# Recurrent core of a two-block mixer kernel: the next chunk's front steps placed between the steps of the present chunk

## What is computed

```
def step(state, inp):
    r_t, w_t, k_t, v_t, kk_t, a_t = inp
    sa = jnp.einsum('bhvk,bhk->bhv', state, kk_t)
    state = (state * w_t[:, :, None, :]
             - sa[..., :, None] * (kk_t * a_t)[..., None, :]
             + v_t[..., :, None] * k_t[..., None, :])
    return state, jnp.einsum('bhvk,bhk->bhv', state, r_t)
...
_, out = lax.scan(step, state0, tuple(seq_first))
```

## Time and profile before

| | |
|---|---|
| median of 3 runs | 2829.52 us (2829.08 to 2830.18) |
| the profiled execution's own time | 2828.0 us |
| its span, first to last instruction | 2826.2 us |
| mean granted TensorE clock | 0.959 |
| TensorE busy, share of the span | 94% |
| VectorE, ScalarE, GpSimd busy | 41%, 20%, 33% |
| the core's matmuls, first to last start | 409.7 to 647.9 us |

### The profile page before, as it was taken

One profiled execution on the slowest core, in us unless ns is written; L12 is line 12 of the kernel. 1 busy time (PEld: TensorE's weight loads), 2 busy tenths in 40 slices (PEclk: granted clock), 3 DMA queues, 4 the chain that ended last, 5 costly groups with the idle time before them and its releaser, 6 DMA issues.

```text
span 2826.2 us, 35717 instructions
## 1 busy us (share of the span) xinstructions
PE 2644.1 (94%) x15644; PEld 1584.4 (56%) x15644; DVE 1151.9 (41%) x1288; ACT 560.9 (20%) x617; POOL 928.9 (33%) x390
## 2 busy tenths in 40 slices
PE   4869999999899999999998899999889999999996
PEld 1545558886455555555554666776345555555552
DVE  5466666663533310223126665255443220222233
ACT  3225422211211100111003122321131110011102
POOL 0212110000144444444445766101124444444450
PEclk8989999999899999999998999998889999999998
DMA  5432020000011111111113412300001111111101
GB/s 237 164 119 82 20 101 3 3 3 15 30 40 50 54 53 43 45 53 45 62 65 137 58 54 67 119 1 23 30 30 45 53 59 46 44 47 53 59 31 60
DMA packets 44267, 162.65 MB, mean 58 GB/s; under 512 B 4560, under 2 KB 14288, under 8 KB 41168
## 3 DMA queue, kind: packets, MB, share of 16 engines
q1 hardware_dynamic: 38496, 151.21, 16.4%
q10 hardware_dynamic: 5616, 9.17, 1.1%
HBM read 147.77 MB, written 12.58 MB: 57 GB/s over the span
## 4 chain that ended last, share of the span: by engine, by line
PE 87%; DVE 6%; DMA 2%; POOL 2%; issue 1%; ACT 1%; SPq 0%; ACTq 0%; DVEq 0%; POOLq 0%
PE pt L918 17%; PE pt L924 17%; PE pt L921 16%; PE pt L1232 13%; PE pt L561 7%; PE pt L411 3%; PE pt L700 2%; PE pt L1930 2%; PE pt L1936 2%; PE pt L1933 2%; PE pt L344 1%; DVE work L532 1%; DMA work<-in_xT 1%; PE pt L397 1%; PE pt L332 1%
## 5 line engine op out<-in xcount | busy, mean ns | idle before, releaser
L889 POOL TENSOR_TENSOR weights_rounded<-work,cst 128x1024 fp32r<-128x1024 f32 (+1 forms) x120 | 314.8, 2623 | 956.9 <-issue 692.5
L921 PE MATMUL pt<-work,weights_rounded 128*128 128x512 bf16 x1408 | 348.8, 384 | 0.0
L893 POOL TENSOR_TENSOR slots<-work,weights_rounded 128x1024 bf16<-128x1024 f32 (+1 forms) x120 | 337.6, 2813 | 9.4
L921 PEld LDWEIGHTS pt<-work,weights_rounded 128*128 128x128 bf16 x1408 | 125.6, 99 | 183.7 <-issue 66.1
L561 PE MATMUL pt<-work 64*64 64x64 f32 (+5 forms) x4512 | 215.3, 247 | 13.4 <-DVE work L532 12.4
L561 PEld LDWEIGHTS pt<-work 64*64 64x64 f32 (+3 forms) x4512 | 196.7, 144 | 32.3 <-DVE work L532 17.2
L918 PE MATMUL pt<-rounded,weights_rounded 128*128 128x512 f32 x704 | 206.1, 428 | 8.8 <-DVE work L1850 5.2
L918 PE MATMUL pt<-rhs_rounded,weights_rounded 128*128 128x512 f32 x704 | 206.2, 428 | 7.8 <-DVE work L815 4.2
L918 PE MATMUL pt<-hidden_rounded,weights_rounded 128*128 128x512 f32 x704 | 207.5, 427 | 0.0
L1006 DVE SCALAR_TENSOR_TENSOR slots<-pt,par,slots 128x1023 f32<-128x1023 f32 x44 | 56.4, 1283 | 315.7 <-ACT slots L992 315.7
L924 PE MATMUL pt<-hidden_rounded,slots 128*128 128x512 bf16 x704 | 179.9, 387 | 0.0
(11 more groups left out here) (330 smaller groups left out, 3495.0 us busy)
## 6 DMA issues: line engine op xcount, KB each, us to landing
work<-in_w_up SPq DMA_DIRECT2D x88, 512.0 KB, 3.6
work<-in_w_mod SPq DMA_DIRECT2D x11, 2048.0 KB, 8.6
work<-in_w_down SPq DMA_DIRECT2D x32, 704.0 KB, 4.0
slots<-in_w_in SPq DMA_DIRECT2D x31, 512.0 KB, 3.7
slots<-in_w_v SPq DMA_DIRECT2D x10, 512.0 KB, 4.0
work<-in_xT ACTq DMA_DIRECT2D x4, 1024.0 KB, 23.1
x_scratch<-work SPq DMA_DIRECT2D x8, 512.0 KB, 2.7
slots<-in_w_out SPq DMA_DIRECT2D x8, 512.0 KB, 3.4
```

What stands on the lines that cost most here:

```text
L889: did(pool, pool.tensor_tensor(w_hi(n, cols).rearrange("p (k n) -> p k n", n=P), w_raw(n, cols).rearrange("p (k n) -> p k n", n=P), const( ...
L893: did(pool, pool.tensor_tensor(w_lo(n, cols), w_raw(n, cols), w_hi(n, cols).bitcast(F32), ALU.subtract), "ffn_w_split")
L921: pe.matmul(out, top_half(w_hi(n, cols))[:, k * P:k * P + P], rhs_lo(k), start=False, stop=False, skip_group_check=True)
```

## The change

The front steps of chunk `c + 1` (transposes, products, first step, values) no longer stand ahead of that chunk as a block. They are issued one pair at a time between the steps of chunk `c`. TensorE's table `beside` says where: transposes of pair 0 behind the x matmuls of level 0, its products behind the t matmuls of level 0, its first step behind those of level 1; pair 1 likewise at levels 2, 2 and 3; pair 2 at level 4 and, its first step, behind step v of the solve. The values stand behind r and g. VectorE's `beside_x` puts the scores copy of pair 0 behind the masks of level 1, its inverse copy behind those of level 2, pair 1's behind those of levels 3 and 4, pair 2's behind level 4.

From chunk 1 on all pairs use `PT[3]` for the front, so a pair's transposes wait for the inverse copy of the pair before (`inverse_set`). Scores, inverses, token-major copies and values get a second buffer; scores of even chunks lie in slots 45, 46 and 30. These held x for the residual sum. So x for tiles 3 to 7 is loaded once chunk 6 is done. GpSimd clears nine slots, after `lg2` instead of `c8`. Chunk 0's front is a block as before. The number of matmuls, copies and predicated copies is unchanged.

```diff
+        CA2 = (45, 46, 30)
...
+        def scores_at(c, i):
+
+            return w((CA2, CA)[c % 2][i])
+
+        def lower_t(c, i, h, rows, q):
+
+            return scores_at(c, i)[rows, h * 512 + 64 * q:h * 512 + 64 * q + 64]
+
+        def scores(c, i, h, n):
+
+            return scores_at(c, i)[:, h * 512 + n * P:h * 512 + n * P + P]
+
+        def inverse(c, i):
+
+            return w(CB_[i])[:, c % 2 * 256:c % 2 * 256 + 256]
...
+        def front(c, i):
+
+            return PT[i] if c == 0 else PT[3]
...
-            pool.wait_ge(E("pt_filled"), place["c8"] + 1)
-            for s in CA + CC:
+            pool.wait_ge(E("pt_filled"), place["lg2"] + 1)
+            for s in CA + CA2 + CD:
                 did(pool, pool.memset(w(s), 0.0), "core_zeroed")
             for c in range(NC):
                 for i in range(3):
-                    if c > 0:
-                        pool.wait_ge(E("y_done"), 3 * (c - 1) + i + 1)
-                    did(pool, pool.tensor_copy(inverse(i).rearrange("p (x n) -> p x n", x=4),
+                    if c >= 2:
+                        pool.wait_ge(E("solve_done"), 9 * (c - 2) + 6 + i + 1)
+                    did(pool, pool.tensor_copy(inverse(c, i).rearrange("p (x n) -> p x n", x=4),
                                                const("unit").unsqueeze(1).to_broadcast([P, 4, 64])), "inverse_unit")
 
...
+                sequence(0, i)
+            values(0)
             for c in range(NC):
                 tt = slice(c * CH, (c + 1) * CH)
+                if c + 1 < NC:
+                    for i in range(3):
+                        sequence(c + 1, i)
...
+                if c + 1 < NC:
+                    values(c + 1)
...
+            def kept(c, i):
+                dve.wait_ge(E("products_done"), 3 * c + i + 1)
+                V_(dve.copy_predicated(heads(scores_at(c, i)), per_head(keep[:, 0:512], 512), heads(front(c, i)[:, :])),
+                   "scores_kept")
+
+            def first(c, i):
+                dve.wait_ge(E("inverse_unit"), 3 * c + i + 1)
+                dve.wait_ge(E("l_done"), 3 * c + i + 1)
+                V_(dve.copy_predicated(heads(inverse(c, i)), per_head(keep[:, 512:640], P),
+                                       heads(front(c, i)[:, :])[:, :, 0:P]), "inverse_set")
+
+            dve.wait_ge(E("core_zeroed"), 9)
             dve.wait_ge(E("keep_in"), 16)
             dve.wait_ge(E("p_end"), 3)
+            for i in range(3):
+                kept(0, i)
+            for i in range(3):
+                first(0, i)
+            beside_x = {1: (kept, 0), 2: (first, 0), 3: (kept, 1), 4: (first, 1)}
             for c in range(NC):
                 tt = slice(c * CH, (c + 1) * CH)
+                more = c + 1 < NC
                 for i in range(3):
                     V_(dve.tensor_scalar(s_scaled(i), state(i), small(PMID + 8 * i + c), None, ALU.mult))
                     V_(dve.tensor_scalar(s_ended(i), s_scaled(i), small(PEND + 8 * i + c), None, ALU.mult), "state_scaled")
...
                 for n, b in enumerate(LEVELS):
                     for i in range(3):
                         dve.wait_ge(E("x_done"), 15 * c + 3 * n + i + 1)
                         V_(dve.tensor_tensor(heads(xbuf(i)), heads(bank_a(i)[:, 0:P]), per_head(const(f"level{b}"), 64),
                                              ALU.mult), "x_masked")
+                    if more and n in beside_x:
+                        step, i = beside_x[n]
+                        step(c + 1, i)
                     for i in range(3):
                         dve.wait_ge(E("t_done"), 15 * c + 3 * n + i + 1)
+                        t = inverse(c, i)
...
+                if more:
+                    kept(c + 1, 2)
+                    first(c + 1, 2)
...
+            def transposes(c, i):
                 tt = slice(c * CH, (c + 1) * CH)
+                if c > 0 and i == 0:
+                    pe.wait_ge(E("mv_kept"), c)
+                if c > 0 and i > 0:
+                    pe.wait_ge(E("inverse_set"), 3 * c + i)
+                for x, s in enumerate((Z + i, B + i, KK + i, VV + i)):
+                    ins = pe.transpose(front(c, i)[:, x * P:x * P + P], w(s)[:, tt], const("ident"))
+                ins.then_inc(E("transposed"), 1)
+
+            def products(c, i):
+                tt = slice(c * CH, (c + 1) * CH)
+                pe.wait_ge(E("seq_major"), 3 * c + i + 1)
+                for x, s in enumerate((B + i, KK + i)):
+                    for h in range(2):
+                        ins = mm(front(c, i)[:, h * 512 + x * 256:h * 512 + x * 256 + 256], w(s)[half(h), tt],
+                                 both(Z, i, 21, tt)[half(h)])
+                ins.then_inc(E("products_done"), 1)
...
+            def first(c, i):
                 tok = [slice(c * CH + 64 * q, c * CH + 64 * q + 64) for q in range(2)]
...
+                pe.wait_ge(E("scores_kept"), 3 * c + i + 1)
...
+                ins.then_inc(E("l_done"), 1)
+
+            def values(c):
                 if c > 0:
-                    pe.wait_ge(E("mv_kept"), c)
...
                 ins.then_inc(E("mv_done"), 1)
+
+            pe.wait_ge(E("pt_emptied_dve"), ordinal["o2"])
+            pe.wait_ge(E("core_zeroed"), 9)
+            for step in (transposes, products, first):
+                for i in range(3):
+                    step(0, i)
+            values(0)
+            beside = {"x0": (transposes, 0), "t0": (products, 0), "t1": (first, 0), "x2": (transposes, 1), "t2": (products, 1),
+                      "t3": (first, 1), "x4": (transposes, 2), "t4": (products, 2), "v": (first, 2)}
+            for c in range(NC):
+
+                def also(phase):
+                    if c + 1 < NC and phase in beside:
+                        step, i = beside[phase]
+                        step(c + 1, i)
+
                 for n in range(5):
                     for i in range(3):
-                        pe.wait_ge(E("inverse_ready"), 18 * c + 3 * n + i + 1)
+                        if n == 0:
+                            pe.wait_ge(E("inverse_set"), 3 * c + i + 1)
+                            if c > 0:
+                                pe.wait_ge(E("o_kept"), 3 * (c - 1) + i + 1)
+                        else:
+                            pe.wait_ge(E("inverse_ready"), 15 * c + 3 * (n - 1) + i + 1)
...
+                    also(f"x{n}")
                     for i in range(3):
                         pe.wait_ge(E("x_masked"), 15 * c + 3 * n + i + 1)
+                        if n == 0 and c > 0:
+                            pe.wait_ge(E("state_new"), 3 * (c - 1) + i + 1)
...
                         ins.then_inc(E("t_done"), 1)
+                    also(f"t{n}")
...
+                    ins.then_inc(E("solve_done"), 1)
+                also("v")
...
                     ins.then_inc(E("rg_done"), 1)
+                if c + 1 < NC:
+                    values(c + 1)
...
                     sp.wait_ge(E("pt_filled"), place["c8"] + 1)
-                    sp.dma_start(W[:, XP[0]:XP[0] + 5, :], a["xT"][:, 0:5, :]).then_inc(E("x_in0"), 16)
-                if m == 1:
-                    sp.wait_ge(E("pt_filled"), place["lg2"] + 1)
-                    sp.dma_start(W[:, XP[5]:XP[5] + 2, :], a["xT"][:, 5:7, :]).then_inc(E("x_in1"), 16)
+                    sp.dma_start(W[:, XP[0]:XP[0] + 3, :], a["xT"][:, 0:3, :]).then_inc(E("x_in0"), 16)
                 if m == 4:
                     sp.wait_ge(E("pt_emptied_dve"), ordinal["bon2"])
                     sp.wait_ge(E("p_end"), 3)
-                    sp.dma_start(w(XP[7]), a["xT"][:, 7, :]).then_inc(E("x_in2"), 16)
                     woc = EX[:, 0:3, :].rearrange("p a n -> p (a n)").rearrange("p (m n) -> p m n", m=8)
                     for mm in range(8):
                         sp.dma_start(woc[:, mm, :], a["w_out"][mm][:, 640:1024]).then_inc(E("woc_in"), 16)
+                    sp.wait_ge(E("chunk_done"), 3 * NC - 3)
+                    sp.dma_start(W[:, XP[3]:XP[3] + 2, :], a["xT"][:, 3:5, :]).then_inc(E("x_in1"), 16)
+                    sp.dma_start(W[:, XP[5]:XP[5] + 2, :], a["xT"][:, 5:7, :]).then_inc(E("x_in2"), 16)
+                    sp.dma_start(w(XP[7]), a["xT"][:, 7, :]).then_inc(E("x_in2"), 16)
             sp.wait_ge(E("y_c"), 3)
             sp.wait_ge(E("pt_filled"), place["o7"] + 1)
```

More of the change, by code:

```diff
@@ L489, in core_act, with sequence @@
         def core_act(act):
-            act.wait_ge(E("core_zeroed"), 6)
+            def sequence(c, i):
+                act.wait_ge(E("transposed"), 3 * c + i + 1)
+                did(act, act.activation(w(CC[i])[:, c % 2 * 512:c % 2 * 512 + 512], front(c, i)[:, 0:512], ACT.Copy),
+                    "seq_major")
+            def values(c):
+                act.wait_ge(E("mv_done"), c + 1)
+                did(act, act.activation(W[:, CD[0]:CD[2] + 1, c % 2 * 512:c % 2 * 512 + P],
+                                        PT[3][:, 512:896].rearrange("p (i n) -> p i n", i=3), ACT.Copy), "mv_kept")
@@ L502, in core_act @@
```

(32 more changed lines are left out.)

115 lines of the change are left out of this document (40 added, 75 removed).

## The result

| | before | changed |
|---|---|---|
| median | 2828.34 us (2823.18 to 2833.87, 8 runs) | 2845.91 us (2839.02 to 2854.58, 8 runs) |
| ratio, 95% interval | | 1.0064 (1.0048 to 1.008) |
| profiled execution: own time, span | 2828.0, 2826.2 | 2846.58, 2844.8 |
| mean granted clock | 0.959 | 0.962 |
| core, first transposes to the last state update's end | 240.3 us | 265.8 us |

The change makes the kernel 17.6 us slower, which is more than the 0.2% that a measurement can tell. A chunk's period is counted from the end of one chunk's last state update to the end of the next one's; the core's first and last chunk are not counted, since the changed order puts the next chunk's front into the first and has none to put into the last.

The account below looks back on a forecast made before the run. The prediction took TensorE to carry 87% of the chain, with levels where TensorE and VectorE are nearly full. Waits +15, tile shapes +4 and clock +7 made +26 us, giving 2855.5 us, range 2835 to 2875.

Parts of the forecast that it names:

- rival (a): Core: slower by waits and shape changes alone, clock at 2.4 GHz throughout; +11 us, 2840; chance 0.18.
- clock term: Core: new waits double the present six stretches at half clock to twelve, 15.6 us against 8.2; +7 us.
- shape term: Core: tile-shape changes on TensorE go from some 7 to 16 a chunk, 0.1 us for each uncovered one; +4 us.
- the sign: Core: the chunk's period away from half clock should be 31 to 31.7 us in the changed profile.
- The waits: Core: TensorE waits for moved VectorE steps in levels, less the front's 2.3 us; +2.15 us a chunk, +15 in all.
- 8.45 end to end: Levels 1 and 2 laid end to end with moved work and waits: 3.35 and 5.1 us, 8.45 together.
- Outside the core: Clearing and late x loads outside the core: 0 us with cover, at most 9 without it.
- (b): Core: faster, moved work fills TensorE's waits, under 2.3 us of added waits per chunk; 2805 us; chance 0.08.

Follow-up runs that it names:

- e1: Changed kernel with VectorE's six state scalings moved from the chunk's head to the solve part: chunk 31.23 us against 32.38, in all 2842.64 us.
- e2: Changed kernel with the transposes of pairs 1 and 2 one step later, their products and pair 2's first step following: chunk 30.09 us, in all 2828.14.
- e3: Changed kernel with scores copies of pairs 0 and 1 cut from 512 to 64 columns per head, chunks 1 to 7: chunk 30.38 us, in all 2829.16.
- e8: Changed kernel with both scalings moved to the solve part and later transposes of pairs 1 and 2: chunk 28.95 us, ratio 0.9966 to the kernel before.
- e4b: Kernel before plus four dummy matmul calls a chunk with 128x128 weights in the solve, chunks 1 to 7: in all 2841.89 us.
- e6: Changed kernel with both order tables rewritten for more lead behind copies, values behind the chunk's last matmul: chunk 28.15 us, ratio 0.9961 to the kernel before.
- e7: Changed kernel with another pair of order tables, values left in place, scalings behind r and g: 2815.53 us, ratio 0.9967 to the kernel before.
- e5: Kernel before with only nine cleared slots instead of six and the late loads of x: chunk 28.94 us, in all 2829.57 beside 2822.03.
- r1: The changed kernel profiled once more, unchanged: total 2856.81 us against 2846.58 in its first profile, core 266.7 us.
- r2: The kernel before profiled once more, unchanged: cores of the two profiles 240.3 and 240.4 us, stages outside the core 2583.1 us.
- e4a: Kernel before plus four dummy matmul calls a chunk with 64x64 weights, the shape around them, chunks 1 to 7: in all 2825.82 us.

## Why the prediction was right, point by point

Slower was forecast at 0.87, 2855.5 us within 2835 to 2875; it is 2845.91, between the forecast and rival (a) at 2840. The mechanism, waits of TensorE for moved VectorE steps, was right. That +26 for the core came so close to its 25.5 was luck: the clock term was 7 us too high and the shape term 5 too low. The chunk's period shows the second, 32.38 us where 31 to 31.7 was given as the sign.

**The waits (+2.15 a chunk, +15).** Right, in place and size. By the timeline they are 1.31, 0.51 and 1.14 us, forecast as 1.4, 0.5 and 1.15, and e1, e2 and e3 take them away one by one (1.15, 2.29 and 2.00 us a chunk, the last with the gaps of 0.2 between x steps, which were forecast too); e8 shows that the first two add. As a net term the 2.15 was not measured by itself: it is the chunk's 3.45 less the 1.3 by which "issue" grew. The argument from the earlier trace rows, two nearly full engines that hand over to each other, is what the runs bear out.

**The tile shapes (+4).** Mis-sized. "Issue" grew by 1.3 us a chunk, 9 us over seven chunks. I had charged 0.1 us for six of nine new changes. By e4b one costs an estimated 0.15, and nine make 1.35. Levels 1 and 2 show it: from 588.76 to 597.67 they take 8.91 us, and I had laid 8.45 end to end; four changes lie there, into and out of the transposes and the products. The wait hides the change into the transposes, but not the one out of them (0.17 at 595.06), and behind lone products the next weight load comes late by 0.33. The row's 0.17 for every change would have been the better estimate. So was the Trainium skill's rule (TensorEngine Tiling (Array Packing), Key Properties) that changing the tiling mode drains TensorE, under which the term was 7.

**The clock (+7).** Wrong. Twelve spells were forecast from the number and length of the waits; there are five, one double, about as much half clock as before (20.5 us in both). Before, the seven counted periods exceed 7 x 28.93 by 8.0 us, in the changed kernel six exceed 6 x 32.38 by 7.5, so the term is near 0. "Each spell at 1.2 GHz came in a chunk whose TensorE had just stood through those waits" was true, but nearly every chunk stands through them, and it does not say which gets a spell: ten of fourteen inverse-copy waits have none, e1 with fewer waits has more half clock, and e2, e3, e6, e7 and e8 have none in the core behind chunk 0. That removing waits removes spells fits these five and not e1, and e4b has more spells without a new wait for another engine, so the cause is open.

**Outside the core (0).** Right for loads and clearing (e5); the changed kernel's clearing and the first unit copies are through by 383.4 us, well ahead of the core. Not foreseen was that unchanged stages would run some 7 us shorter. With 15 + 9 + 0 = 24 for the terms, the core's +25.5 is nearly accounted for, and the total's 17.6 is that less the stages outside. Those took 2585.9 and 2583.1 us in the two profiles of the kernel before and 2579.0 and 2588.3 in those of the changed one (r1 is 31.5 us over r2 in all), so no shift by the change is shown: what differs is mostly their time at half clock. The distance between forecast and median is thus for the most part a matter of stages that the prediction rightly put at no cost, and of their scatter.

**The rivals.** (a), waits without half clock, was close in total for another reason: spells remained, the shapes cost more, and the outside gave something back. (b), faster, was wrong for this table and right for another. Its condition was under 2.3 us of added waits a chunk with the copies in idle VectorE time; e6 and e7 reach it by giving most copies a step of lead, and e8's period, 28.95, only comes back to the kernel before. The passage cited for this rival stands in Perfetto Trace Analysis of the Trainium skill under Optimization Strategy; its advice to interleave came out wrong with this table (32.38 us a chunk) and right with e6's (28.15). I had taken the two full engines of the levels for a reason against any such order, where they spoke against one in which TensorE's next instruction needs the copy just started.

## What to carry to other kernels

Work moved into a stage whose two engines hand over to each other is not hidden by the idle share of either: find for each moved step what its engine's very next instruction waits for, and leave one step of the other work between producer and consumer (e2: 2.29 us a chunk for a table of a few words). Count each change of tile shape, about 0.15 us here, the ones beside a wait too. When stages outside the change scatter by 10 us, read the changed stage's own span and a period away from half clock first.

## What was not expected of the hardware

The half clock repeats: in two profiles of each program the spells stand in the same places of the core, within 0.1 us counted from the core's start (20.5 us at 1.2 GHz each), while the stages outside differ by 24 us of half clock between two runs of one program. And eight small matmul records a chunk changed it: with 64x64 weights (e4a) the amount stayed at 20.5 us, with 128x128 (e4b) it became 37.5, with a spell in each of the chunks 1 to 7, at four changes of shape and 1.6 us more time. Why is open.
